# Up-weights of routed experts as one 8 KB run per partition, with gathered rows turned by every fourth column

## Chip, cores and metric

The kernel runs on one core of a Trainium2 chip. The metric is the device time of one execution in microseconds (us). Three runs of the kernel before gave 1488.46, 1491.83 and 1492.55 us, median 1491.83 us.

## What is computed

The reference is one step of a two-layer trunk over 640 tokens (512 latent and 128 context tokens) of 1024 features in float32. Layer 0 mixes tokens by latent attention and retention, layer 1 by a gated convolution. After each mixing follows a mixture of 32 experts, and only that part is touched by the change. A router picks 2 experts for each token, so 1280 rows go through experts. Cut to what matters:

```
def run(args):                                   # one block of rows, all of one expert
    xb, e = args
    a, b = jnp.split(xb @ w_up[e], 2, axis=-1)   # w_up[e]: 1024 x 512
    return (jax.nn.silu(a) * b) @ w_down[e]      # w_down[e]: 256 x 1024
```

Per layer the up-weights are 32 x 1024 x 512 and the down-weights 32 x 256 x 1024 float32 numbers: 2 MB and 1 MB for an expert.

## The kernel before, in words

**Order of the work.** Token mixing of layer 0, experts of layer 0, token mixing of layer 1, experts of layer 1. The program of each engine is written out by hand, with semaphores between them. The two expert stages lie at about 540 to 780 us and 1199 to 1440 us of the span; after each the rows of the experts are read back and summed per token.

**Rows.** The tokens' features are written to `h_rows` in HBM, two half rows of 512 numbers (2 KB) for a token. An expert's rows are cut into blocks of 64. For each block GpSimd (POOL) gathers 128 half rows by an indirect DMA into one of four places `land` (L2205): partition p holds the first half of row p, partition 64 + p the second half. VectorE (DVE) copies the place to `xrow` (L1950). TensorE (PE) turns it by four transposes of 128 columns each into PSUM (`turn_rows`, L937 to L941); DVE copies the result to `xblk` (L1955), where slice k holds the 128 features that meet row group k of the up-weights. In a transpose the turned data is the stationary operand, so it is read by the weight load (PEld L940), and the identity matrix moves.

**Experts.** For a block, `up` (L943) multiplies the eight slices of `xblk` by the expert's up-weights, two 64-column halves of the array side by side: 16 matmuls that the profile shows as 32 records of L955. Then come the four transposes of the next block, the eight records of the block before in `down` (L977), one transpose of the gated hidden values (`turn`, L965), and the next `up`. ScalarE (ACT) and DVE do the gate (L1443, L1516), ACT takes the result (L1454), and POOL scatters 128 half rows of it to `y_rows` (L2210). POOL's loop for a block waits for the gathered rows and gives a tick (L2200), waits for ACT's result, copies the two columns of indices, issues the gather two blocks ahead and the scatter of this block, and then waits until the scatter of the block before has landed (`freed`, which gives the other tick of L2200).

**Weights.** SyncE (SP) loads an expert by three DMAs of 1 MB: two of up-weights, 512 rows each (L488), and one of down-weights (L491), into three slots of 8 KB per partition. There are six such places. `refill` (L512 to L519) first waits until PE has done the last `up` of expert e, issues the two up-loads of expert e + 6 into its slots, then waits for its last `down` and issues the down-load. SP's DMAs go to one hardware queue, in the order of issue; POOL's go to a software queue; both are served by the same 16 DMA engines. PE waits for each of the three slots before it first reads it (L952, L971).

Before the change, partition p of an up-slot holds rows p, 128 + p, 256 + p and 384 + p of its 512 rows, four runs of 2 KB. A down-slot has two runs of 4 KB. The modulation weights `ada_w`, loaded in the first 250 us, are rows of 8 KB, one for a partition.

Of the kernel before, what the change touches and what calls it, by code (L numbers as in the profile page):

```python
# [12 lines left out]
P = 128  # L13
# [135 lines left out]
def build(nc, io):  # L149
    f = io  # L150
    ctx = ExitStack()
    with ctx:
# [3 lines left out]
        def sem(name):  # L156
            return ctx.enter_context(nc.semaphore(name))
# [42 lines left out]
        ident = cst[:, C_ID:C_ID + P]  # L200
# [50 lines left out]
        xrow = arena[:, A_XROW:A_XROW + HALFROW]  # L251
# [7 lines left out]
        def slot(s):  # L259

            if s < SLOTS:
                return ring[:, s, :]
            return arena[:, A_SLOT + (s - SLOTS) * SLOT:A_SLOT + (s - SLOTS + 1) * SLOT]
# [48 lines left out]
        ring_full = [sem(f"ring_full{s}") for s in range(SLOTS + MORE)]  # L312
        S = {}

        def ev(name):
            if name not in S:
                S[name] = sem(name)
            return S[name]
# [66 lines left out]
        def quad(b):  # L385
            return PS[:, b, :].rearrange("p (j n) -> p j n", j=4)
# [21 lines left out]
        def turned_bank(u):  # L408

            return 4 + 2 * (u % 2)  # L410
# [17 lines left out]
        def _(sp):  # L428
# [54 lines left out]
            def load_part(l, e, j, s):  # L483

                if j < 2:
                    src = f["moe_w_up"][l, bass.ds(e, 1), 512 * j:512 * j + 512, :] \
                        .rearrange("e (k p) n -> p (e k) n", p=P)
                    sp.dma_start(slot(s).rearrange("p (k n) -> p k n", k=4), src).then_inc(ring_full[s], 16)  # L488
                else:
                    src = f["moe_w_down"][l, bass.ds(e, 1), :, :].rearrange("e (k p) n -> p (e k) n", p=P)  # L490
                    sp.dma_start(slot(s).rearrange("p (k n) -> p k n", k=2), src).then_inc(ring_full[s], 16)  # L491

            def load_experts(l):
# [18 lines left out]
                def refill(e, p):  # L512

                    done = expert_done(e)
                    sp.wait_ge(ev(f"up_mm{l}"), done)
                    for j in range(2):
                        load_part(l, e + NPLACE, j, PLACES[p][j])
                    sp.wait_ge(ev(f"down_mm{l}"), done)
                    load_part(l, e + NPLACE, 2, PLACES[p][2])  # L519
# [12 lines left out]
            n = 0  # L532
# [16 lines left out]
        def _(pe):  # L549
# [55 lines left out]
            for g, r in enumerate(V_ROWS):  # L605
                last = pe.transpose(PS[:, 5, g * P:g * P + r], vrow[0:r, g, :], cst[0:r, C_ID:C_ID + r])
            last.then_inc(ev("vec_t"), 1)

            for i in range(2 * NT):
# [5 lines left out]
                for j in range(4):  # L615
                    last = pe.transpose(quad(i % 4)[:, j, :],
                                        xtok[:, t, (4 * half + j) * P:(4 * half + j + 1) * P], ident)
# [152 lines left out]
            for u in range(len(UNITS) + 2):  # L770
# [4 lines left out]
                if u < len(UNITS):  # L775
# [7 lines left out]
                    for half in range(2):  # L783
                        if kind == "q":
                            for k in range(2):
                                last = pe.matmul(PS[:, b + half, 0:384], cT[:, t, k, :],
                                                 wq[:, k, half * 384:half * 384 + 384],
                                                 start=(k == 0), stop=(k == 1))
                        else:
                            lat = cT[:, t, 2, :] if t < NT else cache_cT[:, :]  # L790
                            last = pe.matmul(PS[:, b + half, :], lat, wkv[:, half * 512:half * 512 + 512],
                                             start=True, stop=True)
                    last.then_inc(ev("qk_mm"), 1)
                if u >= 2:
# [10 lines left out]
                    for h in range(HEADS):  # L805
                        last = pe.transpose(quad(turned_bank(u - 2) + h // 4)[0:QK, h % 4, :], raw[:, h, :], ident)
# [7 lines left out]
            for i in range(NATT + 3):  # L814
                if i < NATT:
# [4 lines left out]
                    if kind == "lat":  # L820
                        for n in range(2):
                            last = pe.matmul(PS[:, b + n, 0:SEG], qT[:, h, t * P:t * P + P],  # L822
                                             kT[:, h, n * SEG:(n + 1) * SEG], start=True, stop=True)
                    else:
                        for n in range(4):
                            last = pe.matmul(quad(b)[:, n, :], qT[:, 4 * h + n, SAMPLE:T],
                                             kT[:, 4 * h + n, 640:768], start=True, stop=True)
                    last.then_inc(ev("s_mm"), 1)
                if 2 <= i <= NATT + 1:
# [6 lines left out]
                    for j in range(ST + 1 if kind == "lat" else 4):  # L836
                        last = pe.transpose(quad(4 + j // 4)[:, j % 4, :], prob[i % 2][:, j, :], ident)
                    last.then_inc(ev("p_t"), 1)
                if i - 3 in GROUP_END:
# [5 lines left out]
                    for pair in (range(2) if g < 2 else (0,)):  # L845
                        for j in range(ST + 1 if g >= 2 else 1):
                            for hl in range(2):
                                if g < 2:
                                    h = 4 * g + 2 * pair + hl
                                    out = PS[hl * VD:(hl + 1) * VD, 6 + g % 2, pair * P:(pair + 1) * P]  # L850
                                    last = pe.matmul(out, vS[:, 5, h, :],
                                                     probT[0][:, g, (2 * pair + hl) * P:(2 * pair + hl + 1) * P],
                                                     start=True, stop=True)
                                else:
                                    last = pe.matmul(PS[hl * VD:(hl + 1) * VD, 6 + g % 2, :],
                                                     vS[:, j, 2 * (g - 2) + hl, :], probT[hl][:, j, :],
                                                     start=(j == 0), stop=(j == ST))
# [3 lines left out]
            for t in range(NT):  # L861
# [4 lines left out]
                for j in range(4):  # L866
                    last = pe.transpose(quad(t % 4)[:, j, :], oret[:, t, j * P:(j + 1) * P], ident)
# [6 lines left out]
            def moe(l):  # L874
# [5 lines left out]
                for k in range(KD):  # L880
                    for n in range(2):
                        pe.wait_ge(ev("h_s"), KD // 2 + KD * (q - 1) + k + 1)
                        if n == 1:
                            pe.wait_ge(ev("h_c"), KD * (q - 1) + k + 1)
                        last = pe.matmul(PS[0:ROUTE, 5 * n, 0:SEG], wr[:, k, :], hT[:, k, n * SEG:(n + 1) * SEG],
                                         start=(k == 0), stop=(k == KD - 1))
# [24 lines left out]
                for i in range(2 * NT):  # L911
# [3 lines left out]
                    for j in range(4):  # L915
                        last = pe.transpose(quad((1, 2, 3, 7)[i % 4])[:, j, :],
                                            hT[:, 4 * half + j, t * P:t * P + P], ident)
# [7 lines left out]
                for j in range(2 * NT):  # L925
                    for h in range(2):
                        last = pe.matmul(PS[h * BLK:(h + 1) * BLK, 6, 0:NB], hot_lo[:, j, :], hot_hi[:, j, :],
                                         start=(j == 0), stop=(j == 2 * NT - 1))
# [6 lines left out]
                def turn_rows(n):  # L935

                    pe.wait_ge(ev(f"x_taken{l}"), n + 1)  # L937
                    pe.wait_ge(ev(f"xblk_c{l}"), n + 1)
                    for m in range(4):
                        last = pe.transpose(quad(3)[:, m, :], xrow[:, m * P:(m + 1) * P], ident)  # L940
                    last.then_inc(ev(f"rows_t{l}"), 1)  # L941

                def up(n, p, laps):  # L943
# [54 lines left out]
                def laps_at(g):  # L998

                    return lambda c: g * 16 + full_count[n0 + c]  # L1000

                turn_rows(0)
                up(0, 0, laps_at(0))
                with pe.Fori(0, rounds) as g:
# [117 lines left out]
            for k in range(KD):  # L1122
                pe.wait_ge(ev("ln_sq"), k + 1)
                for t in range(NT):
                    c = t * P if t < ST else CTX0
                    last = pe.matmul(PS[:, 0, t:t + 1], cv2[:, k, c:c + P], ones[:, 0:1],
                                     start=(k == 0 and t == 0), stop=(k == KD - 1 and t == NT - 1))
# [1210 lines left out]
```

## Time and profile before

| what | value |
|---|---|
| runs | 1488.46, 1491.83, 1492.55 us |
| the profiled execution's own time | 1487.51 us |
| its span, first to last instruction | 1485.7 us |
| mean granted TensorE clock | 0.941 |
| PE busy | 1285.3 us (87%) |
| DVE, ACT, POOL busy | 581.2, 296.3, 303.7 us |
| DMA packets, bytes | 149095, 322.65 MB |
| shares of the chain that ended last | PE 52%, DVE 15%, SP's queue 14%, DMA 7%, issue 7% |

The profile's times are of one execution. A share of an engine is an average over the whole span, and the stages have different limits, so the stages are read one by one. The "DMA share" of a stretch is the mean busy share of the 16 DMA engines; transfers that overlap on one engine can make it pass 1.

### The profile page before, as it was taken

The page shows a single profiled execution, that of the slowest core. Times are in us where ns is not written, and L with a number is a line of the kernel's source. Part 1 is how long each engine was busy: PE and PEld are TensorE (multiplying, and loading weights), DVE is VectorE, ACT ScalarE, POOL GpSimd, SP SyncE. Part 2 cuts the span into 40 slices and gives each one's busy share as a digit, 9 for nine tenths or more (in the row PEclk, how much of TensorE's full clock was granted, in tenths as well). Part 3 has the DMA queues.
Part 4 walks back from the last instruction along what each step waited for, and adds up shares of the span by engine and source line. Part 5 has one row for each costly group of instructions (what it writes and reads, how often), then busy time and mean ns, then how long its engine had stood idle before and what let it go on. Part 6 is the DMA issues. An engine that isn't in the chain of part 4 may idle for free.

```text
span 1485.7 us, 21303 instructions
## 1 busy us (share of the span) xinstructions
PE 1285.3 (87%) x7165; PEld 820.4 (55%) x7166; DVE 581.2 (39%) x1371; ACT 296.3 (20%) x653; POOL 303.7 (20%) x703
## 2 busy tenths in 40 slices
PE   4999998878799769997775899999898779999776
PEld 3666775554467445543334767666676445555336
DVE  1211433665422442221111379999412522222213
ACT  3300045554400311111111300000311311111110
POOL 3000100300000023443332211250000034444330
PEclk9999999979999769999997899999699679999998
DMA  9565645310061169999994811100071279999975
GB/s 339 232 277 230 267 180 230 122 55 1 1 255 57 71 208 401 412 408 400 404 356 167 246 57 31 54 29 0 0 278 62 89 270 398 386 400 411 404 281 218
DMA packets 149095, 322.65 MB, mean 217 GB/s; under 512 B 16182, under 2 KB 49948, under 8 KB 142884
## 3 DMA queue, kind: packets, MB, share of 16 engines
q1 hardware_dynamic: 128432, 288.25, 51.1%
q0 software_dynamic: 12464, 21.91, 4.2%
q10 hardware_dynamic: 8131, 11.57, 2.2%
q8 instruction: 45, 0.74, 0.2%
q14 instruction: 23, 0.18, 0.0%
HBM read 312.41 MB, written 27.08 MB: 229 GB/s over the span
## 4 chain that ended last, share of the span: by engine, by line
PE 52%; DVE 15%; SPq 14%; DMA 7%; issue 7%; ACT 3%; POOL 2%; ACTq 1%; POOLq 0%; DVEq 0%
PE PS L599 10%; PE PS L648 8%; DVE arena L2055 8%; PE PS L955 7%; SPq L491 7%; SPq L488 5%; PE PS L977 3%; DMA ring<-in_moe_w_up 3%; PE PS L1023 3%; PE PS L570 3%; PE PS L1082 2%; PE PS L822 2%; DVE scratch L1516 2%; DVE arena L1516 2%; PE PS L1099 2%
## 5 line engine op out<-in xcount | busy, mean ns | idle before, releaser
L1516 DVE TENSOR_TENSOR arena<-arena,PS 128x128 f32<-128x128 f32 (+1 forms) x101 | 33.4, 349 | 313.2 <-ACT arena L1443 304.2
L955 PE MATMUL PS<-arena 128*64 128x256 f32 x1152 | 134.7, 383 | 21.7 <-DMA arena<-in_moe_w_up 20.8
L2055 DVE SCALAR_TENSOR_TENSOR arena<-arena,vecT 128x655 f32<-128x655 f32 x181 | 151.0, 907 | 0.0
L955 PE MATMUL PS<-ring,arena 128*64 128x256 f32 x1056 | 129.0, 395 | 22.6 <-DMA ring<-in_moe_w_up 20.9
L599 PE MATMUL PS<-arena,ring 128*128 128x320 f32 x512 | 142.3, 442 | 5.7 <-DVE arena L1792 3.7
L1082 PE MATMUL PS<-arena,ring 128*128 128x320 f32 x512 | 141.4, 437 | 3.3 <-issue 2.2
L648 PE MATMUL PS<-ring,arena 128*128 128x256 f32 (+1 forms) x640 | 140.3, 372 | 0.0
L648 PEld LDWEIGHTS PS<-ring,arena 128*128 128x128 f32 x640 | 114.7, 190 | 26.7 <-issue 13.4
L599 PEld LDWEIGHTS PS<-arena,ring 128*128 128x128 f32 x512 | 99.4, 194 | 48.2 <-issue 8.9
L1082 PEld LDWEIGHTS PS<-arena,ring 128*128 128x128 f32 x512 | 98.3, 192 | 45.3 <-issue 5.6
L955 PEld LDWEIGHTS PS<-arena 128*64 128x64 f32 x1152 | 80.1, 137 | 65.1 <-DMA arena<-in_moe_w_up 17.5
L955 PEld LDWEIGHTS PS<-ring,arena 128*64 128x64 f32 x1056 | 76.3, 141 | 65.6 <-DMA ring<-in_moe_w_up 18.5
L1443 ACT ACTIVATE arena<-PS 128x128 f32<-128x128 f32 x69 | 19.1, 277 | 274.8 <-PE PS L955 274.8
L977 PE MATMUL PS<-arena 128*64 128x512 f32 x288 | 69.7, 605 | 1.5 <-ACT arena L1454 1.5
L2210 POOL DMA_INDIRECT y_rows<-arena,scatter_col x64 | 65.1, 1018 | 22.5 <-issue 22.5
L2281 POOL TENSOR_SCALAR arena<-cst,vecT 128x128 f32<-128x128 f32 x51 | 41.5, 830 | 124.3 <-PE PS L1099 124.3
L2100 POOL TENSOR_SCALAR arena<-arena,modA,modT 128x128 f32<-128x128 f32 x24 | 10.7, 449 | 274.2 <-DVE arena L1516 274.2
L1454 ACT ACTIVATE arena<-PS 128x512 f32 x61 | 36.4, 597 | 147.3 <-PE PS L977 147.3
L1023 PE MATMUL PS<-scratch,arena 128*128 128x128 f32 x320 | 42.1, 297 | 27.1 <-DMA arena<-y_rows 27.1
L2196 POOL TENSOR_TENSOR pool_tick<-cst 128x1 f32<-128x1 f32 x128 | 24.7, 193 | 198.5 <-ACT arena L1454 193.4
L2205 POOL DMA_INDIRECT arena<-h_rows,gather_col x56 | 59.3, 1058 | 28.3 <-issue 28.3
L977 PE MATMUL PS<-ring,arena 128*64 128x512 f32 x264 | 63.9, 605 | 0.0
(324 smaller groups left out, 1623.3 us busy)
## 6 DMA issues: line engine op xcount, KB each, us to landing
ring<-in_moe_w_up SPq DMA_DIRECT2D x64, 1024.0 KB, 13.8
arena<-in_moe_w_up SPq DMA_DIRECT2D x64, 1024.0 KB, 13.6
ring<-in_ada_w SPq DMA_DIRECT2D x48, 1024.0 KB, 10.9
ring<-in_moe_w_down SPq DMA_DIRECT2D x32, 1024.0 KB, 15.2
arena<-in_moe_w_down SPq DMA_DIRECT2D x32, 1024.0 KB, 15.2
arena<-y_rows ACTq DMA_DIRECT2D x10, 1024.0 KB, 11.1
ring<-in_od_w_in SPq DMA_DIRECT2D x16, 512.0 KB, 6.2
ring<-in_ev_w_in SPq DMA_DIRECT2D x7, 1024.0 KB, 14.9
```

The lines of the kernel that those rows point to most:

```text
L488: sp.dma_start(slot(s).rearrange("p (k n) -> p k n", k=4), src).then_inc(ring_full[s], 16)
L491: sp.dma_start(slot(s).rearrange("p (k n) -> p k n", k=2), src).then_inc(ring_full[s], 16)
L599: last = pe.matmul(PS[:, b + n, 0:SEG], w[:, k, c:c + P], src[:, tile(k), n * SEG:(n + 1) * SEG], start=(k == 0), stop=(k == KD - 1))
L648: last = pe.matmul(z_bank(i)[:, 0:n], hT[:, k, t * P:t * P + P], w[:, k, 0:n], start=(k == 0), stop=(k == KD - 1))
L955: last = pe.matmul(PS[i * BLK:(i + 1) * BLK, 0, 0:2 * P].rearrange("p (a n) -> p a n", a=2), xblk[:, k, :], w[:, k % 4, :, i * P:(i + 1) * P],
L977: last = pe.matmul(PS[c * BLK:(c + 1) * BLK, 2, :], hblk[:, i, :], w[:, i, c * 512:(c + 1) * 512], start=(i == 0), stop=(i == 1))
L1023: last = pe.matmul(quad(4 + i % 4)[:, m, :], ygat[:, t, a, c:c + P], wdiag[:, a, t, :], start=(a == 0), stop=(a == 1))
L1082: last = pe.matmul(PS[:, 2 * a + n, 0:SEG], w[:, k, a, :], hT[:, k, n * SEG:(n + 1) * SEG], start=(k == 0), stop=(k == KD - 1))
L1516: return dve.tensor_tensor(out, a, b, op)
L2055: dve.scalar_tensor_tensor(out=acc, in0=src, scalar=wc, in1=acc, op0=ALU.mult, op1=ALU.add).then_inc(ev("conv_v"), 1)
L2205: pool.indirect_dma_start(land[r], None, h_rows[:, :], bass.IndirectOffsetOnAxis(ap=col, axis=0), bounds_check=2 * T - 1, oob_is_err=False ...
L2210: pool.indirect_dma_start(y_rows[:, :], bass.IndirectOffsetOnAxis(ap=col, axis=0), yblk[r], None, bounds_check=2 * ROWS - 1, oob_is_err=Fa ...
```

## The change

An up-slot's partition p now holds rows 4p to 4p + 3 of its 512 rows, which stand next to each other in HBM: one run of 8 KB. The 1 MB of a DMA is then one piece of HBM. For the products to stay what they are, slice m of a block has to hold the features 4c + m instead of 128m + c, so each transpose reads every fourth column of `xrow`. Nothing else is changed: the same number of DMAs, bytes, transposes and matmuls, and the same waits.

```diff
@@ load_part (SP)
                 if j < 2:
                     src = f["moe_w_up"][l, bass.ds(e, 1), 512 * j:512 * j + 512, :] \
-                        .rearrange("e (k p) n -> p (e k) n", p=P)
-                    sp.dma_start(slot(s).rearrange("p (k n) -> p k n", k=4), src).then_inc(ring_full[s], 16)
+                        .rearrange("e (p k) n -> p (e k n)", p=P)
+                    sp.dma_start(slot(s), src).then_inc(ring_full[s], 16)
@@ turn_rows (PE)
                     for m in range(4):
-                        last = pe.transpose(quad(3)[:, m, :], xrow[:, m * P:(m + 1) * P], ident)
+                        last = pe.transpose(quad(3)[:, m, :], xrow.rearrange("p (c m) -> p m c", m=4)[:, m, :], ident)
                     last.then_inc(ev(f"rows_t{l}"), 1)
```

## Rows read from the trace of the kernel before

**Rows 1.** Windows: busy time (instructions) per engine, granted clock, DMA share, GB/s.
```profile
580.00:660.00 80.00, 80.00 (x576) 41.41 (x574) 19.97 (x51) 11.86 (x38) 39.59 (x104) 1.00 1.04 410
660.00:760.00 100.00, 74.96 (x510) 37.23 (x508) 18.06 (x47) 11.29 (x35) 34.23 (x93) 1.00 1.04 401
...
1220.00:1260.00 40.00, 40.00 (x294) 20.88 (x292) 9.51 (x24) 5.79 (x18) 16.82 (x40) 1.00 1.03 392
1340.00:1380.00 40.00, 40.00 (x292) 20.64 (x290) 9.51 (x24) 5.79 (x18) 19.78 (x53) 1.00 1.04 410
1380.00:1420.00 40.00, 30.83 (x210) 14.88 (x208) 7.92 (x20) 4.82 (x15) 14.42 (x40) 1.00 1.04 405
```

**Rows 2.** Groups of instructions, PE line L955: busy, mean ns, idle before, releasers.
```profile
L955 PE MATMUL PS<-arena 128*64 128x256 f32 x1152 | 134.7, 383 | 21.7 <-DMA arena<-in_moe_w_up 20.8 <-DVE arena L1955 0.9
L955 PE MATMUL PS<-ring,arena 128*64 128x256 f32 x1056 | 129.0, 395 | 22.6 <-DMA ring<-in_moe_w_up 20.9 <-issue 1.7
```

**Rows 3.** The chain that ended last, in order of time: start, us, what.
```profile
577.17 1.89 PE PS L977 x8
579.22 3.08 SPq L491
...
762.75 15.50 DMA arena<-in_moe_w_up
778.29 1.95 PE PS L955 x16
...
1320.28 4.65 SPq L491
```

**Rows 4.** Timeline of SP, the last down-load issued in each expert stage.
```profile
765.47 3.55 SPq L491 DMA_DIRECT2D arena<-in_moe_w_down  x1
...
1425.55 3.47 SPq L491 DMA_DIRECT2D arena<-in_moe_w_down  x1
```

**Rows 5.** Windows in which runs of one length alone are loaded (columns as rows 1).
```profile
145.00:155.00 10.00, 10.00 (x60) 7.04 (x59) 2.62 (x6) 0.38 (x1) 0.00 (x0) 1.00 1.01 424
...
298.00:300.00 2.00, 1.05 (x8) 0.83 (x8) 1.43 (x4) 1.25 (x4) 0.00 (x0) 0.90 1.04 403
300.00:302.00 2.00, 0.42 (x2) 0.44 (x3) 2.00 (x3) 0.70 (x2) 0.00 (x0) 0.50 1.01 412
437.00:441.00 4.00, 4.00 (x17) 2.81 (x16) 0.00 (x0) 0.00 (x0) 0.00 (x0) 1.00 1.00 372
441.00:443.00 2.00, 2.00 (x9) 1.42 (x8) 0.55 (x2) 0.00 (x0) 0.00 (x0) 1.00 1.06 430
549.00:553.00 4.00, 4.00 (x32) 2.23 (x30) 1.30 (x3) 0.28 (x1) 0.63 (x1) 1.00 1.04 400
```

**Rows 6.** Page, part 3, SP's and POOL's queue: packets, MB, share of 16 engines.
```profile
q1 hardware_dynamic: 128432, 288.25, 51.1%
q0 software_dynamic: 12464, 21.91, 4.2%
```

**Rows 7.** Line L940, the weight loads of the transposes: ns min/median/max, first and last start.
```profile
L940 PEld LDWEIGHTS PS<-cst,arena x284: 137/140/230, 537.8 to 1440.1; 128*128 128x128 f32 x142
```

**Rows 8.** Windows around the first of these transposes (columns as rows 1).
```profile
537.00:539.00 2.00, 1.09 (x4) 0.71 (x4) 0.47 (x2) 0.00 (x0) 1.36 (x3) 0.50 0.00 0
```

**Rows 9.** Timeline of POOL, one block of layer 0.
```profile
620.53 1.02 POOL L2210 DMA_INDIRECT y_rows<-arena,scatter_col  x1 [0.30 <-issue]
621.57 0.35 POOL L2200 TENSOR_TENSOR pool_tick<-cst 128x1 f32<-128x1 f32 x2
624.27 0.19 POOL L2196 TENSOR_TENSOR pool_tick<-cst 128x1 f32<-128x1 f32 x1 [2.35 <-ACT arena L1454]
...
627.88 0.35 POOL L2200 TENSOR_TENSOR pool_tick<-cst 128x1 f32<-128x1 f32 x2
```

**Rows 10.** Line L2210, the scatters: issue to landing.
```profile
DMA to landing us min/median/max: 2.1/5.8/7.8
```

**Rows 11.** Line L2106, POOL's small loads beside the first 4 and 8 KB runs.
```profile
DMA to landing us min/median/max: 6.7/8.7/9.6
```

## The prediction

> **What bounds the kernel now.** The page first: PE is busy for 87% of the span, but that mixes stages, so I went to windows of the two expert stages, the only ones the change touches. From 580 to 660 us PE is busy without a gap and the DMA engines are full too (share 1.04, 410 GB/s). From 660 to 760 us the DMA engines stay full and PE is busy 75 of 100 us. Layer 1 shows the same later: PE has no gap up to 1380 us and then 9 us of gaps in 40 [rows 1]. The groups of instructions name what PE waits for: in front of the up matmuls it idles 20.8 + 20.9 = 41.7 us for `moe_w_up` [rows 2]. 25 us of gaps lie between 660 and 760 us, 9 us between 1380 and 1420 [rows 1], and the rest right behind these, so some 29 us in layer 0 and 12.7 us in layer 1. The chain of waits gives the start: up to 579 us it runs through PE, from there through SP's issues, which are held back by a full queue, to the landing of the last up-weights at 778.3 us, where PE takes them at once; in layer 1 it leaves PE at 1320 us [rows 3]. So both stages begin bound by PE (6.32 us a block: POOL's tick comes at 621.57 and 627.88 [rows 9]) and end bound by the DMA engines. SP's timeline has 21 down-loads after 579.2 us, the last at 765.5 us, and 12 after 1320.3 us, the last at 1425.6 us [rows 3, 4]: they come 8.9 and 8.8 us apart on average.
>
> **Part 1, the up-loads.** 128 loads of 1 MB keep their bytes; 512 packets each become 128, so SP's queue drops from 128432 packets [rows 6] by 128 x 384 = 49152 to about 79280. What a packet costs comes from stretches in which one length of run is loaded. 2 KB runs: 403, 372 and 400 GB/s; 4 KB runs: 412 and 430; 8 KB runs of `ada_w`: 424 [rows 5]. I take 400, 412 and 424, because they rebuild the stage: 2.097 MB at 400 is 5.24 us, 1.049 MB of down-weights at 412 is 2.55 us, and POOL's queue, 21.91 MB over 64 experts [rows 6] or 0.34 MB for one, takes 0.84 us at 400: 8.63 us, against 3.49 MB / 401 = 8.70 by the stage's own rate [rows 1]. With 8 KB runs the up part is 2.097 / 424 = 4.95 us, **0.30 us less for an expert** that the DMA engines bound. Bounds: if the whole loss of 401 against 424 GB/s over 3.49 MB lay in the up-runs, they would give back 8.70 - 8.23 = 0.47 us, of which I keep 0.43, since the 4 KB runs lose some too. Below, the stage shows 410 with the same mix while PE is full [rows 1]; a fixed cost per packet that fits 410 and 424 is some 4 ns, times 48 fewer packets on each engine, 0.19 us. Zero, or a loss, is a rival.
>
> The Trainium skill (DMA: Bandwidth & Descriptors, Why small descriptors are slow) gives about 3 cycles a packet beside one cycle per 32 bytes. By it, as an estimate, an up-load would go from 67/64 to 259/256 of its ideal time, 3.4% less, or 0.18 us an expert. No row here shows that mechanism by itself.
>
> Which experts count? Those that the DMA engines bound: 21 in layer 0 and 12 in layer 1, and in each the two whose loads are queued at the turning point (a load lands 15.5 us after its issue [rows 3], close to two services): 23 + 14 = 37. Bounds 33 (none of the queued) and 42 (share 1.03 already from 1220 us [rows 1], which the faster engines would partly turn into idle time). **37 x 0.30 = 11.1 us**; from 33 x 0.19 = 6 to 42 x 0.43 = 18. It can't be eaten by the floor beneath: layer 0 would lose 6.9 of 29 us of PE gaps, layer 1 4.2 of 12.7. At the end nothing new is late, as the last up-load is still followed by the same matmuls, scatter and read-back.
>
> SP issues as many DMAs as before. Their long issue times are the full queue's; with a quarter of the packets I expect SP to be held back less and more bytes to stand in the queue, so that issue to landing may get longer than now. That costs nothing: the order in the queue is the same, and an expert's slots are free when SP issues. The first six experts of a stage are loaded long before they are needed, so their gain is nothing.
>
> **Part 2, the transposes.** There are 2208 / 32 = 69 blocks [rows 2], 33 in layer 0 and 36 in layer 1, with four transposes each, and what is strided is the weight load: 128 numbers per partition at a step of 16 bytes. A load takes 140 ns now [rows 7]. No row shows a strided float32 operand on PE. From below the price is zero (a gain has no source: same bytes, same count). From above: the slowest load, 230 ns [rows 7], is of the first block, where the granted clock is 0.50, that is 1.2 GHz [rows 8]; a load whose reads go at half rate can hardly lose more than one that goes at half clock, 90 ns. Times four that is 0.36 us a block. It lies on the path only where PE bounds: (579 - 540) / 6.32 = 6 blocks of layer 0 and (1320 - 1199) / 6.32 = 19 of layer 1. That is 25 x 0.36 = 9.0 us at most; in the other blocks the gaps in front of the up matmuls cover it, and without that cover all 69 blocks would pay 25 us. I take zero: nearest are the plain loads of the same line at full clock, and the 140 ns hold more than the reading of 128 columns (they don't double at half clock).
>
> **Sum.** 0 to 9 us for the transposes, 11.1 off for the loads. On the profiled execution 1487.5 - 11 = 1476.5 us. That execution lies 4.3 us below the median of the three runs, and the sum applied to the median gives **1481 us**. Its own range is 1474 to 1486.
>
> **Rivals.**
> *The strided loads go at half rate.* For it: every column lies 16 bytes from the next. Against it: nothing in the trace. The price is between 4.4 us (half of the bound) and 9.0, so the change gains 2 to 7 us: 1487, range 1484 to 1490. At over 0.44 us a block, 110 ns a load, it would eat the whole gain. The Trainium skill (SBUF — State Buffer, Door 1) speaks against this change: lines of SBUF are 16 bytes, and at least two reads of each line are needed for full rate, where a step of four float32 numbers gives one. By that rule, this rival is the result.
>
> *Not the packet's length but the memory limits the rate.* For it: 2 and 4 KB runs overlap (403 and 412), one 4 KB stretch reaches 430, beyond the 8 KB runs [rows 5]. The `ada_w` rows come from other addresses than one solid megabyte. Then the change does not do what it says: 1492, or 1491 to 1497 with a part of the transposes' price.
>
> *Slower: the software queue is starved.* An engine that takes turns between queues waits longer behind an 8 KB packet. Scatters land in 5.8 us beside the weights and in 2.1 us at best [rows 10], so the neighbours cost 3.7 us. The mean packet of SP's queue takes (64 x 82 + 16 x 159) / 80 = 97 ns on an engine now and (16 x 309 + 16 x 159) / 32 = 234 ns after, 2.4 times. If the extra scales with it, a scatter lands after 2.1 + 8.9 = 11.0 us. POOL's slack is 9.7 us: 7.35 from the issue at 620.53 to the tick at 627.88, which waits for nothing, and 2.35 in which it then idles for ACT [rows 9]. From 9.7 us on POOL sets the pace. I take 0.8 us a block, a landing of 10.5 us, between the slack and that: layer 1 becomes 36 x 7.12 = 256 us against its 241 now, and layer 0, 33 x 7.12 = 235 and 2 for the first block at 1.2 GHz, against 240: 12 us slower, 1504. Below about 0.5 us a block, a landing of 10.2 us, the gain of layer 0 makes up for layer 1. Against it: POOL's small loads beside 4 and 8 KB runs at the start took 8.7 us, at most 9.6, with others of their own queue ahead of them [rows 11]; and landings in the expert stages vary little though 2 and 4 KB runs alternate. The Trainium skill (DMA: Bandwidth & Descriptors, Queues, rings and completion order) has each engine change queues at packets only, which is the rule behind this rival.
>
> **Chances.** Forecast 0.50, half-rate loads 0.25, rate unchanged 0.15, starved software queue 0.10. A measurement of this kernel tells about 0.3%, 4.5 us, from no change. Faster by more: 0.48 of the forecast and 0.11 of the second. Within it: 0.02, 0.14 and 0.12. Slower: 0.03 and 0.10. The range runs from the forecast's lower end over the half-rate and most of the unchanged case, 1474 to 1493.
>
> **What would show it.** SP's queue with about 79280 packets. In 660:760 us some 415 GB/s, and down-loads 8.3 us apart. The gaps for `moe_w_up` near 31 us instead of 41.7. PEld of L940 at 140 ns; 180 to 230 is the half-rate rival, with blocks of 6.5 to 6.7 us while PE is full. Scatters landing under 9.7 us; above, POOL idles in front of its tick L2200 for `y_rows`. The prediction is wrong if up-loads alone don't pass 410 GB/s, or if a stage without gaps on PE gets longer.

## The result, and the profile after

The changed kernel takes 1480.63 us in the median of five runs (1476.77 to 1482.74), the kernel before 1492.55 us beside it (1488.46 to 1495.46, five runs). The ratio is 0.9916, with a 95% interval of 0.9895 to 0.9937: **some 12 us faster** (11.9 by the medians, 12.5 by the ratio). The profiled execution took 1476.77 us (span 1474.9) where the one of before took 1487.51.

The page of after, part 3, for the two queues of [rows 6] (packets, MB, share of 16 engines):

```profile
q1 hardware_dynamic: 79280, 288.25, 49.3%
q0 software_dynamic: 12464, 21.91, 4.2%
```

49152 packets are gone from SP's queue, the bytes are the same, and the same bytes took less of the engines' time: 51.1% before. The windows of after that answer to [rows 1], with a new one for 1260 to 1300 us:

```profile
580.00:660.00 80.00, 80.00 (x571) 42.53 (x567) 19.26 (x48) 11.83 (x38) 38.55 (x102) 1.00 1.02 422
660.00:760.00 100.00, 82.32 (x554) 42.47 (x552) 20.55 (x51) 11.86 (x37) 37.64 (x99) 1.00 1.02 423
...
1260.00:1300.00 40.00, 40.00 (x284) 21.29 (x282) 9.91 (x25) 6.06 (x19) 19.57 (x50) 1.00 0.95 367
1340.00:1380.00 40.00, 40.00 (x283) 21.25 (x283) 9.92 (x25) 6.47 (x20) 18.54 (x50) 1.00 1.02 423
1380.00:1420.00 40.00, 34.04 (x235) 17.30 (x231) 8.02 (x20) 4.82 (x15) 16.35 (x43) 1.00 1.02 422
```

Where the DMA engines are full they now move 422 to 423 GB/s, whatever PE does; before it was 401 to 410. That is the rate of the 8 KB `ada_w` runs, 424 [rows 5]. PE is busy 82.3 us of the hundred where it was 75.0. What it still waits for stands in the groups of L955 (busy, mean ns, idle before), against 20.8 and 20.9 us for `moe_w_up` in [rows 2]:

```profile
L955 PE MATMUL PS<-arena 128*64 128x256 f32 x1152 | 134.2, 383 | 13.0 <-DMA arena<-in_moe_w_up 11.8 <-DVE arena L1955 1.1
L955 PE MATMUL PS<-ring,arena 128*64 128x256 f32 x1056 | 126.1, 389 | 17.5 <-DMA ring<-in_moe_w_up 15.9 <-issue 1.7
```

The gaps fell from 41.7 to 27.7 us. The transposes' line shows the other side (ns min/median/max); [rows 7] had 137/140/230:

```profile
L940 PEld LDWEIGHTS PS<-cst,arena x284: 195/212/226, 538.7 to 1430.3; 128*128 128x128 f32 x142
```

A weight load with a step of 16 bytes takes 212 ns, 72 ns more. It is hidden in part: POOL's timeline of after, to be read beside [rows 9], has its ticks 6.42 and 6.38 us apart where they were 6.31.

```profile
615.96 0.34 POOL L2200 TENSOR_TENSOR pool_tick<-cst 128x1 f32<-128x1 f32 x2
618.75 0.19 POOL L2196 TENSOR_TENSOR pool_tick<-cst 128x1 f32<-128x1 f32 x1 [2.45 <-ACT arena L1454]
...
621.33 1.02 POOL L2210 DMA_INDIRECT y_rows<-arena,scatter_col  x1 [0.30 <-issue]
622.38 0.34 POOL L2200 TENSOR_TENSOR pool_tick<-cst 128x1 f32<-128x1 f32 x2
...
628.76 0.36 POOL L2200 TENSOR_TENSOR pool_tick<-cst 128x1 f32<-128x1 f32 x2
```

So a block costs PE 0.09 to 0.10 us more (four loads of 72 ns would be 0.29; two thirds lie beside matmuls). The tick at 622.38 still follows the scatter's issue at once, and POOL still idles 2.45 us for ACT: the scatters are not late here. Over both expert stages, POOL waited for a scatter's landing in front of L2200 three times, 1.5 us in all, where it was twice and 0.7 us before.

The chain that ended last (start, us, what) leaves PE later than in [rows 3], at 611.5 instead of 579.2 us, and in layer 1 at 1344.6 instead of 1320.3:

```profile
609.45 1.89 PE PS L977 x8
611.50 1.89 SPq L491
...
748.04 23.67 DMA arena<-in_moe_w_up
771.76 1.95 PE PS L955 x16
...
1344.60 2.23 SPq L488
...
1379.82 24.68 DMA ring<-in_moe_w_up
```

The last up-load of layer 0 lands at 771.8 us (778.3 before). It takes 23.7 us from issue to landing instead of 15.5: at 423 GB/s that would be 10.0 MB ahead of it in the queue, against 6.2 MB at 401 (an estimate, rate times time).

**The stages in numbers.** The chain gives two marks for each layer: the router's matmuls L927 in front of the experts and the sums L1023 behind them. First before, then after:

```profile
527.05 2.41 PE PS L927 x40
803.05 9.85 PE PS L1023 x64
1186.01 2.41 PE PS L927 x40
1455.11 9.79 PE PS L1023 x64
```

```profile
528.88 2.41 PE PS L927 x40
796.62 8.89 PE PS L1023 x64
1181.18 2.42 PE PS L927 x40
1445.38 8.78 PE PS L1023 x64
```

From L927 to L1023 layer 0 goes from 276.0 to 267.7 us, layer 1 from 269.1 to 264.2: **8.3 and 4.9 us**, together 13.2. The other stretches, which the change does not touch, add up to 2.4 us more in this execution (1.8 before the first mark, 1.6 between the layers, 1.1 less at the end). Over the ten other profiles of this study whose code there is the same, the first mark lies between 530.2 and 533.2 us, so a few us in one execution mean nothing there; the two stage lengths are the better measure, and I use them below. They have noise too: where two or three profiles have the same code in a layer, the lengths differ by 0.4 to 1.4 us, and once, with one of the doubled kernels below, by 2.2. So a difference of about 1 us between two single profiles says little.

### The profile page after: what moved, and what is told of

Its sections match the earlier page's. It is cut to its first block, busy times and chain, and to the rows that moved or that the text cites. A ratio compares the mean times of both kernels' runs of the same rounds, so it can differ in the third digit from the quotient of the medians.

```text
span 1474.9 us, 21303 instructions
## 1 busy us (share of the span) xinstructions
PE 1289.7 (87%) x7165; PEld 831.6 (56%) x7166; DVE 582.5 (39%) x1371; ACT 296.3 (20%) x653; POOL 304.0 (21%) x703
## 3 DMA queue, kind: packets, MB, share of 16 engines
q1 hardware_dynamic: 79280, 288.25, 49.3%
## 4 chain that ended last, share of the span: by engine, by line
PE 57%; DVE 15%; SPq 9%; DMA 8%; issue 6%; ACT 3%; POOL 2%; ACTq 1%; POOLq 0%; DVEq 0%
PE PS L599 10%; PE PS L955 9%; PE PS L648 8%; DVE arena L2055 8%; SPq L488 5%; PE PS L977 4%; DMA ring<-in_moe_w_up 3%; SPq L491 3%; PE PS L1023 3%; PE PS L570 3%; PE PS L1082 2%; PE PS L822 2%; PE PS L940 2%; DVE scratch L1516 2%; DMA arena<-in_moe_w_up 2%
## 5 line engine op out<-in xcount | busy, mean ns | idle before, releaser
L955 PE MATMUL PS<-arena 128*64 128x256 f32 x1152 | 134.2, 383 | 13.0 <-DMA arena<-in_moe_w_up 11.8
L955 PE MATMUL PS<-ring,arena 128*64 128x256 f32 x1056 | 126.1, 389 | 17.5 <-DMA ring<-in_moe_w_up 15.9
L955 PEld LDWEIGHTS PS<-arena 128*64 128x64 f32 x1152 | 80.3, 137 | 55.5 <-DMA arena<-in_moe_w_up 10.9
L955 PEld LDWEIGHTS PS<-ring,arena 128*64 128x64 f32 x1056 | 75.1, 139 | 58.8 <-DMA ring<-in_moe_w_up 13.9
L977 PE MATMUL PS<-arena 128*64 128x512 f32 x288 | 69.7, 605 | 1.5 <-ACT arena L1454 1.5
L2210 POOL DMA_INDIRECT y_rows<-arena,scatter_col x64 | 65.1, 1018 | 22.4 <-issue 22.4
L940 PE MATMUL PS<-cst,arena 128*128 128x128 f32 x284 | 53.8, 313 | 14.9 <-DVE arena L1950 14.9
L1023 PE MATMUL PS<-scratch,arena 128*128 128x128 f32 x320 | 41.8, 296 | 27.2 <-DMA arena<-y_rows 27.2
L977 PE MATMUL PS<-ring,arena 128*64 128x512 f32 x264 | 63.9, 605 | 0.0
```

Of the source, the lines that this page charges most:

```text
L940: last = pe.transpose(quad(3)[:, m, :], xrow.rearrange("p (c m) -> p m c", m=4)[:, m, :], ident)
L955: last = pe.matmul(PS[i * BLK:(i + 1) * BLK, 0, 0:2 * P].rearrange("p (a n) -> p a n", a=2), xblk[:, k, :], w[:, k % 4, :, i * P:(i + 1) * P],
L977: last = pe.matmul(PS[c * BLK:(c + 1) * BLK, 2, :], hblk[:, i, :], w[:, i, c * 512:(c + 1) * 512], start=(i == 0), stop=(i == 1))
L1023: last = pe.matmul(quad(4 + i % 4)[:, m, :], ygat[:, t, a, c:c + P], wdiag[:, a, t, :], start=(a == 0), stop=(a == 1))
L2210: pool.indirect_dma_start(y_rows[:, :], bass.IndirectOffsetOnAxis(ap=col, axis=0), yblk[r], None, bounds_check=2 * ROWS - 1, oob_is_err=Fa ...
```

## The experiments

Three questions were open. Does the gain come from the packet's length or from the solid megabyte? What does the strided read cost, and on which stretch is it paid? And which resource sets the end of a stage in which PE and the DMA engines are both full? None leaves any of the computation out; two do transposes twice. The kernel before was measured beside each set of kernels: 1492.17 us beside the first four (23 runs), 1493.74 beside the next four (11 runs), 1492.77 beside the last two (21 runs). "+/-" gives a 95% interval of a difference of means.

### The order made by VectorE

```diff
@@ take_landed (DVE), on the changed kernel
-                    dve.tensor_copy(xrow, src)
+                    dve.tensor_copy(xrow.rearrange("p (m c) -> p m c", m=4),
+                                    src.rearrange("p (c m) -> p m c", m=4))
@@ turn_rows (PE)
-                        ... xrow.rearrange("p (c m) -> p m c", m=4)[:, m, :], ident)
+                        ... xrow[:, m * P:(m + 1) * P], ident)
```

> The kernel after, but DVE's copy of the gathered rows (L1950) puts every fourth column side by side, so that the transposes read 128 columns in one run again; 8 KB runs as after. Theory A, the strided weight load costs PE 0.09 us a block (a block takes 6.41 us after, 6.32 before) and only the PE-bound blocks count (about 29 to 45 of 69): 3 to 4 us faster than after, 14 to 16 us faster than before, L940's loads back at 140 ns and a block at 6.32 us. Theory B, the load's extra 72 ns are hidden behind the other operand's work and the 0.09 us come from something else: no change against after, 12 us faster than before. In both DVE's copy may take 0.2 to 0.4 us longer, beside DVE's idle time.

Measured: 1479.46 us (1476.69 to 1481.87, six runs), ratio 0.9916 (0.9901 to 0.9931). Its line L940 and its groups of L955 (one line lower in the code):

```profile
L940 PEld LDWEIGHTS PS<-cst,arena x284: 137/140/230, 542.0 to 1432.4; 128*128 128x128 f32 x142
```

```profile
L955 PE MATMUL PS<-arena 128*64 128x256 f32 x1152 | 134.5, 383 | 16.7 <-DMA arena<-in_moe_w_up 15.9 <-DVE arena L1956 0.9
L955 PE MATMUL PS<-ring,arena 128*64 128x256 f32 x1056 | 126.0, 389 | 18.2 <-DMA ring<-in_moe_w_up 16.1 <-issue 2.2
```

The loads are back at 140 ns, the block at 6.32 us, so the strided load is where the 0.09 us came from, against theory B. DVE's copy L1950 went from a mean of 421 to 624 ns, and no wait for it grew (PE 15.3 us in all, at the first blocks of the two stages, where it was 16.9 in the kernel before). The median is 1.2 us under the changed kernel's, too little to tell the two theories' times apart. The gaps for up-weights are 32.0 us instead of 27.7: of the 69 x 0.09 = 6.2 us that PE saves, 4.3 turn into waiting. Layer 0's stage is 267.6 us long, as in the changed kernel, and layer 1's 263.3 instead of 264.2.

### The stride alone

```diff
@@ take_landed (DVE), on the kernel before: loads stay four runs of 2 KB
-                    dve.tensor_copy(xrow, src)
+                    dve.tensor_copy(xrow.rearrange("p (c m) -> p m c", m=4),
+                                    src.rearrange("p (m c) -> p m c", m=4))
@@ turn_rows (PE)
-                        ... xrow[:, m * P:(m + 1) * P], ident)
+                        ... xrow.rearrange("p (c m) -> p m c", m=4)[:, m, :], ident)
```

> The kernel before, with its 2 KB runs, but the transposes read every fourth column (DVE's copy spreads the rows so that the products stay the same). Theory A: the stride alone makes a block 6.41 us where PE has no gap, that is 25 to 30 blocks on the path: 2 to 3 us slower than before, 1494 to 1496 us, and the DMA engines stay at 401 to 410 GB/s. Rival (half-rate loads at the full price of 0.29 to 0.36 us a block): 7 to 9 us slower. Rival (hidden): same as before.

Measured: 1493.69 us (1490.9 to 1496.14, twelve runs), ratio 1.001 (1.0001 to 1.002), so 1.5 us slower, and no more than 3. L940 loads take 212 ns here too. Layer 0's stage is 276.3 us (276.0 before), layer 1's 270.3 (269.1). The 25 blocks that the prediction counted as bound by PE, at 0.09 us each, would be 2.3 us, inside the interval. The full price of 0.29 to 0.36 us a block is not.

### Short packets over the same megabyte

```diff
@@ load_part (SP), on the changed kernel
-                        .rearrange("e (p k) n -> p (e k n)", p=P)
-                    sp.dma_start(slot(s), src)
+                        .rearrange("e (p k) n -> p (e k) n", p=P)
+                    sp.dma_start(slot(s).rearrange("p (k n) -> p k n", k=4)[:, ::-1, :], src)
@@ turn_rows (PE)
-                        ... [:, m, :], ident)
+                        ... [:, 3 - m, :], ident)
```

The four rows of a partition are written in reverse order, so that a packet can't be longer than 2 KB though the addresses read are those of the changed kernel.

> The kernel after with the same bytes in the same partitions, but each partition's 8 KB taken as four runs of 2 KB (their order in the slot reversed, so that they can't be joined, and the transposes reversed with it). Theory A, what is gained is the packets' fixed cost: SP's queue has 128432 packets again, the full stretches fall from 423 back to 400 to 410 GB/s, and the time is that of before plus the stride's 2 to 3 us, 1494 us. Rival, the addresses make it (one solid megabyte instead of rows 256 KB apart): 423 GB/s and 1481 us in spite of the packets.

Measured: 1491.82 us (1489.91 to 1496.47, twelve runs), ratio 1.0001 (0.9988 to 1.0013). Its queue and windows:

```profile
q1 hardware_dynamic: 128432, 288.25, 50.6%
```

```profile
580.00:660.00 80.00, 80.00 (x559) 41.88 (x555) 20.48 (x51) 11.85 (x37) 36.54 (x96) 1.00 1.04 411
660.00:760.00 100.00, 79.29 (x540) 41.11 (x540) 19.26 (x48) 11.58 (x36) 36.55 (x96) 1.00 1.04 404
```

**The gain is gone**, with the rates of before. The packet's length makes it, not where the bytes lie. A us or two may still come from the solid megabyte: the kernel with the stride alone, which like this one reads every fourth column, took 1493.69 us, in the means 1.1 +/- 1.6 us more, and its stages are 276.3 and 270.3 us long against 274.7 and 269.4 here. That is not shown.

### Two runs of 4 KB

```diff
@@ load_part (SP), on the changed kernel
-                        .rearrange("e (p k) n -> p (e k n)", p=P)
-                    sp.dma_start(slot(s), src)
+                        .rearrange("e (k p j) n -> p (e k) (j n)", k=2, j=2)
+                    sp.dma_start(slot(s).rearrange("p (k n) -> p k n", k=2), src)
@@ turn_rows (PE)
-                        ... xrow.rearrange("p (c m) -> p m c", m=4)[:, m, :], ident)
+                        ... xrow.rearrange("p (k c j) -> p k j c", k=2, j=2)[:, m // 2, m % 2, :], ident)
```

> Up-weights as two runs of 4 KB per partition; the transposes read every second column, a step of 8 bytes. Theory A, a fixed cost per packet: from 2 to 8 KB an engine's 64 packets of an expert's up-weights become 16 and 0.45 us are saved, so with 32 packets two thirds, 0.30 us: full stretches near 415 to 418 GB/s, 4 us slower than after by the loads. Rival, packets pay only beyond 4 KB or only up to 4 KB: 403 or 423 GB/s. For the stride: if a line of 16 bytes must be hit twice, a step of 8 bytes is free and L940's loads take 140 ns and a block 6.32 us; if the load time grows with the step, some 165 to 175 ns and 6.36 us.

Measured: 1481.87 us (1477.04 to 1482.92, six runs), ratio 0.9925 (0.9908 to 0.9941). Windows and the line of the transposes:

```profile
580.00:660.00 80.00, 80.00 (x560) 41.93 (x561) 20.86 (x52) 12.21 (x38) 36.57 (x96) 1.00 1.03 419
660.00:760.00 100.00, 81.00 (x552) 41.93 (x548) 19.25 (x48) 11.63 (x37) 38.23 (x101) 1.00 1.03 418
```

```profile
L940 PEld LDWEIGHTS PS<-cst,arena x284: 194/209/226, 541.9 to 1434.0; 128*128 128x128 f32 x142
```

4 KB runs bring most of it: 401 to 418 GB/s, then 423 with 8 KB. The time can't be told from the changed kernel's (1480.63). And a step of 8 bytes costs a load 209 ns, as good as a step of 16.

### The down-weights as one 8 KB run too, and the step that it needs

```diff
@@ load_part (SP), on the kernel with DVE's order
-                    src = f["moe_w_down"][...].rearrange("e (k p) n -> p (e k) n", p=P)
-                    sp.dma_start(slot(s).rearrange("p (k n) -> p k n", k=2), src)
+                    src = f["moe_w_down"][...].rearrange("e (p k) n -> p (e k n)", p=P)
+                    sp.dma_start(slot(s), src)
@@ up (PE): the moving operand takes every second column
-                        w = slot(s[k // 4]).rearrange("p (k a n) -> p k a n", k=4, a=2)
+                        w = slot(s[k // 4]).rearrange("p (k a n i) -> p k a i n", k=4, a=2, i=2)
-                                xblk[:, k, :], w[:, k % 4, :, i * P:(i + 1) * P],
+                                xblk[:, k, :], w[:, k % 4, :, i, :],
```

> DVE's copy orders the columns as in e1_dve_order, and the down-weights too land as one 8 KB run per partition; the up matmuls then read every second column of the up-weights as their moving operand, so that slice k of the hidden values meets rows 2p + k. SP's queue should show 79280 - 16384 / 2 = 71088 packets. If packet length goes on paying above 4 KB, the expert stages go from 423 to about 425 GB/s where the DMA engines are full, 0.04 us for an expert and 1 to 2 us in all, if the strided moving operand is free. Theory one (the gain is used up near 4 KB, as 419 GB/s with 4 KB up-runs and 423 with 8 KB suggest, and a strided moving operand costs nothing that PE cannot hide): 1478 to 1480 us, the same as with contiguous transposes alone. Rival (the moving operand is read at a lower rate at a step of 8 bytes): the up matmuls of 256 columns go from about 0.24 us for two to more, 16 of them for each block; at 0.02 us each that is 0.3 us for each of some 25 blocks that PE bounds, or 8 us, 1487 us.

The second kernel keeps the step but writes the down-weights' two rows in swapped order, so the packets stay at 4 KB, and `down` reads them swapped:

> As f1_down_8k, with the down-weights in the same layout but written as two 4 KB runs per partition in swapped order, so that packets stay at 79280 and only the moving operand's step is new against e1_dve_order. If the strided moving operand is free: 1479 us, as e1_dve_order, and the difference of f1_down_8k to this one is the packets' alone. If it costs something, both kernels show it alike in the mean ns of L955 and in the block's period while PE is full.

Measured: 1479.46 us (1476.63 to 1484.41, six runs), ratio 0.9906 (0.9883 to 0.9929), with the 8 KB down-runs (71088 packets); 1483.36 us (1478.26 to 1486.87, six runs), ratio 0.993 (0.9906 to 0.9954), with the step alone (79280). The window of 660 to 760 us, first with both and then with the step alone:

```profile
660.00:760.00 100.00, 85.30 (x573) 41.27 (x569) 23.39 (x52) 12.54 (x39) 39.41 (x104) 1.00 1.01 425
```

```profile
660.00:760.00 100.00, 84.65 (x569) 40.79 (x567) 23.29 (x52) 12.56 (x39) 38.79 (x104) 1.00 1.02 423
```

Neither theory holds alone. The packets pay a little if at all (425 against 423 GB/s; stages 1.0 and 0.7 us shorter, the whole kernel 3.1 +/- 3.6 us in the means), and the step is not free: `down` L977 comes every 6.49 us instead of 6.32 while PE is full, 0.17 us a block, and the stages are 1.2 and 2.4 us longer than the mean of the two profiles with DVE's order. The kernel with the step alone is 5.7 +/- 3.1 us slower than DVE's order measured beside it (1477.16, next section), the one with both 2.5 +/- 3.0. So the kernel is no better than the one that it was built on.

### Both candidates once more, on the same chip

> The kernel of e1_dve_order once more, beside the changed kernel on the same chip, since the two differ by less than one measurement tells. If the strided weight loads lie on the path of some 25 to 35 blocks at 0.09 us, this kernel is 2 to 3 us faster than the changed one. If PE only arrives earlier at weights that have not landed, the difference is under 1 us.

> The changed kernel once more, on the same chip as the three others: 1480.6 us again. It is what f3_dve_order_again is compared with: 2 to 3 us slower than that one if the strided loads lie on the path, within 1 us if not.

Measured: 1477.16 us (1476.09 to 1479.33, five runs), ratio 0.9893 (0.9871 to 0.9915), with DVE's order; 1479.72 us (1477.95 to 1482.93, six runs), ratio 0.9911 (0.989 to 0.9933), changed kernel. All runs of each kernel together: mean 1478.5 (11 runs) against 1480.4 (11 runs). With a spread of about 1.9 us in either group the difference is 1.9 us, give or take 1.7. The six and five runs made side by side give 2.9 +/- 2.2. **DVE's order is the fastest version found**, by about 2 us. The stages don't show where: averaged over two profiles of each, layer 0 loses 0.7 us (268.3 against 267.6) and layer 1 gains 0.9 (263.0 against 263.9), 0.2 together, and the profiled executions themselves average 1478.0 and 1478.3 us.

### Twice the transposes, one layer at a time

```diff
@@ turn_rows (PE), on the changed kernel; in the other kernel l == 1
-                    for m in range(4):
+                    for m in [m for _ in range(2 if l == 0 else 1) for m in range(4)]:
```

> The changed kernel, with the four transposes of a block done twice over in layer 0: the same results are written again, so each block of layer 0 costs PE 0.66 to 0.75 us more (the quad takes 0.75). Theory one: a stage's end is set by the DMA engines from the moment their share stays at 1 or above, in layer 0 from about 565 us, although PE has no gap until 607. Then only the 3 or 4 blocks before that count, which release the first new loads: +2 to +3 us, layer 0's expert stage 267.6 to some 270, and the rest of the cost vanishes as smaller gaps in front of the up matmuls. Theory two: PE sets the end until the chain of waits leaves it at 609 us: 11 blocks, +7 to +8 us.

> The same doubling in layer 1 alone. There the DMA share is 0.92 to 0.97 between 1260 and 1300 us and stays at 1.02 from 1300 on, so PE's pace sets when SP may load until then. Theory one: the 17 blocks between 1193 and 1300 us count at 0.66 to 0.75 us, +11 to +13 us, layer 1's stage 264 to some 276, a little less if the share reaches 1 earlier or later by it. Theory two: 23 blocks until the chain leaves PE at 1340 us, +15 to +17 us. Common to both theories and telling against a third (transposes are never on the path): layer 1 pays far more for the same instructions than layer 0.

Measured: layer 0 doubled 1486.26 us (1482.47 to 1490.83, ten runs), ratio 0.9964 (0.995 to 0.9978); layer 1 doubled 1492.12 us (1488.04 to 1496.3, twelve runs), ratio 0.9998 (0.9985 to 1.0011). So 6 and 12 us more than the changed kernel. PE's timeline with layer 0 doubled shows what it costs a block:

```profile
605.55 1.94 PE L977 MATMUL PS<-arena 128*64 128x512 f32 x8
612.44 1.94 PE L977 MATMUL PS<-arena 128*64 128x512 f32 x8
```

6.89 us instead of 6.41: 0.48 us for four more transposes, not the 0.66 to 0.75 that both theories were given (part of a transpose hides behind its neighbours when eight come in a row). The marks of both, first layer 0 doubled:

```profile
531.57 2.41 PE PS L927 x40
803.30 10.05 PE PS L1023 x64
```

```profile
1183.64 2.41 PE PS L927 x40
1458.69 10.14 PE PS L1023 x64
```

Layer 0's stage takes 271.7 us, 4.0 more than the 267.7 that it takes in the twin kernel where only layer 1 is doubled. Layer 1's takes 275.1, 11.1 more than the mean of 264.2 and 263.6. If every block paid, it would be 33 x 0.48 = 16 and 36 x 0.48 = 17 us. Layer 0 pays for 8 blocks, layer 1 for 23.

For layer 0 that lies between the theories: one had 3 to 4 blocks, 1.4 to 1.9 us at the measured 0.48, and two had 11, 5.3 us. The whole kernel's 6.2 +/- 2.3 us over the changed kernel run again excludes the first count and not the second. The 8 fit the windows if "full" is read by the rate and not by the share, a reading made after the result: 377 GB/s from 560 to 580 us in this kernel, 424 from 580. About 0.6 us of the 4.0 come behind the last landing (25.5 us from there to L1023 instead of 24.9), and the seven blocks left end at 541.5 + 7 x 6.89 = 590 us.

What speaks against theory two is where the chain leaves PE in these two profiles. With layer 1 doubled, layer 0 runs the changed kernel's own code, and its stage is 267.7 us long as there, but the chain stays with PE until 663 us instead of 611:

```profile
657.00 1.87 PE PS L977 x8
659.13 3.95 PE PS L955 x32
664.68 2.47 SPq L488
```

A point that moves by 52 us and leaves the stage's length as it is does not mark the start of the critical stretch. With layer 0 doubled the chain leaves PE at 676.6 us, 20 blocks after the start, and 20 x 0.48 = 9.4 us is more than either measure shows.

For layer 1 neither count can be read off as it was meant, because the doubling moves the point itself:

```profile
1260.00:1300.00 40.00, 40.00 (x291) 22.86 (x289) 9.37 (x24) 5.64 (x18) 18.40 (x48) 1.00 0.93 355
1340.00:1380.00 40.00, 40.00 (x286) 22.28 (x286) 9.34 (x23) 5.52 (x17) 17.45 (x48) 1.00 1.02 423
1380.00:1420.00 40.00, 40.00 (x284) 22.38 (x282) 9.63 (x24) 5.79 (x18) 17.36 (x47) 1.00 1.02 423
```

PE has no gap up to 1420 us and the DMA engines run below capacity until 1320. The 11.1 us are the 17 minus some 6 us of gaps that the doubling filled (PE idles 6.0 us between 1380 and 1420 us in the changed kernel). What stands: the same extra instructions cost nearly three times as much in layer 1 as in layer 0 by the stages, and twice as much by the whole kernel (12.0 against 6.2 us).

The doubled layer 0 leaves 2 us unexplained: its run is some 6 us longer and its stage 4.0. In its profile the untouched stage of layer 1 took 265.8 us, where the changed kernel's two profiles have 264.2 and 263.6. The cause stays open.

## Why the prediction was right, and where its steps were off

The prediction was 1481 us, the measurement 1480.63; the forecast drop was 11.1 us, the measured one 11.9. Part of that agreement is luck: two errors against each other.

**What bounds the kernel.** Right in kind: the gain lies in the expert stages (8.3 and 4.9 us), and it comes from the stretches where the DMA engines are full.

**Packets.** 79280, as counted.

**0.30 us for an expert: too small.** The step that was off is the term "400, 412 and 424". The text expected some 415 GB/s between 660 and 760 us and gaps for `moe_w_up` near 31 us; it got 423 and 27.7. An expert's 3.49 MB take 8.25 us at 423 GB/s. Against the 8.70 us at 401 that is 0.45 us less, beyond the text's own upper bound of 0.43. Against the 8.51 us at 410, which held in the first 80 us, it is 0.26. The text kept some of the loss for the 4 KB down-runs, but those lose almost nothing: with the down-runs at 8 KB as well the rate rises only from 423 to 425. The four lengths give the price of a packet in place of that sum. Removing 32, 16 and 8 packets on each engine for an expert took the stage from 410 to 419, 422 and 424 GB/s where PE is full, which is 0.18, 0.06 and 0.04 us: 4 to 6 ns a packet, near the 4 ns that the text had fitted for its lower bound. Between 660 and 760 us the first step, from 2 to 4 KB, brought 0.35 us, 11 ns a packet. Why 2 KB packets lose more there (401 to 404 GB/s in three kernels, share 1.04) is open.

The rule of the Trainium skill (DMA: Bandwidth & Descriptors, Why small descriptors are slow) gave 0.18 us an expert as an estimate. The right direction, and less than the 0.26 to 0.45 us measured here.

**37 experts: near enough, for another reason than given.** The text started the count where the chain of waits leaves PE. The chain left PE 32 and 24 us later after the change, yet the gain did not shrink, and that point moves by itself, as the doubling shows. What fits is a count from when the DMA engines of the changed kernel run at capacity: about 580 us in layer 0, 1300 in layer 1, PE's gaps or not. These starts were read off after the result. Then the bytes alone give the gain. In layer 0 the kernel before moved 80 us x 410 + 100 us x 401 = 72.9 MB between 580 and 760 us; at 422.6 GB/s that takes 172.5 us, 7.5 less, and some 0.8 for the 18 us to the last landing: 8.3, as measured. In layer 1, if one starts at 1300 us, the kernel before moved 390 and 412 GB/s for 20 us each (its windows below) and 410 and 405 for 40 us each. That is 48.6 MB, 5.0 us less at 423, and some 0.8 to 1440 us: 5.8. Measured were 4.9 with the stride and 6.1 with DVE's order.

```profile
1300.00:1320.00 20.00, 20.00 (x142) 9.90 (x138) 5.22 (x13) 2.89 (x9) 9.22 (x24) 1.00 1.03 390
1320.00:1340.00 20.00, 20.00 (x146) 10.46 (x146) 5.05 (x13) 3.58 (x11) 9.20 (x25) 1.00 1.05 412
```

The kernel before does not show that start: its share is 1.02 or more from 1220 us on. Counted from there, with 373, 411, 401 and 376 GB/s up to 1300 us, the gain would be 12 us, twice what was measured. Only in the changed kernel do the engines fall below capacity from 1260 to 1300 us (share 0.95), probably because the faster engines then wait for PE's pace: with PE slowed by the doubling in layer 1 they stay below it until 1320 us. The prediction had that in its upper bound of 42 experts.

**SP held back less, landings longer.** Right: 23.7 and 24.7 us against 15.5.

**Transposes at zero: wrong in kind, small in effect.** The text took 140 ns, "nearest are the plain loads of the same line"; they took 212. That is most of the way to the bound of 230, and the load does not hide: 0.09 us a block while PE is full. The half-rate rival asked for a block of 6.5 to 6.7 us and got 6.41. What kept it cheap is the second half of the bound, the 25 blocks: about 8 of layer 0 count, as doubling them shows, and PE's loss elsewhere only fills gaps. By price, 8 + 17 blocks at 0.09 us (the 17 being those of layer 1 up to 1300 us) would be 2.3 us; the whole-kernel comparison gives 1.9 +/- 1.7 us, the stride alone on the kernel before 1.5. The stage lengths give 0.2 in the first comparison and 1.5 in the second.

**Sum.** In place of -11.1 and 0: about -14 for the loads (8.3 + 5.8, an estimate), +1 to +2 for the stride; the median fell by 12 (1492.55 to 1480.63).

**The rivals.** *Half-rate loads:* the loads took 212 ns, inside the 180 to 230 of this rival; the time did not follow. The rule behind it (the Trainium skill, SBUF — State Buffer, Door 1: at least two reads of each 16-byte line for full rate) does not fit the runs: a step of 8 bytes makes two reads of a line and costs 209 ns, a step of 16 makes one and costs 212; contiguous is 140. *Rate unchanged:* refuted by the 8 KB rows, and its argument (addresses) by the short packets over the same megabyte. *Starved software queue:* refuted as a cause of time. POOL's tick follows the scatter's issue at once, and it still idles 2.45 us for ACT. So the scatters land inside the 9.7 us of slack, but for the few waits of 1.5 us in all, though the mean packet beside them is 2.4 times as long by the prediction's estimate. The rule behind it (the Trainium skill, DMA: Bandwidth & Descriptors, Queues, rings and completion order: an engine changes queues at packets only) may hold; no run here shows it by itself.

## What to carry to other kernels

Where the windows show the DMA engines full, count packets first: going from 2 KB to 4 KB runs was worth 2 to 4% of the rate, 4 to 8 KB one more per cent. If the layout then asks for a permutation, look for an engine with slack in a copy that is done anyway; here DVE's copy took it for 200 ns that no wait grew by. And when two resources are both full, don't take the start of the critical stretch from the chain of waits: it moved by 52 us here between two executions whose stage was equally long. Price the stretch by bytes over rate, and keep a wide range for where it starts, since that depends on where the changed kernel first runs at its capacity, which the kernel before need not show.

## What the runs showed of the hardware that was not expected

- A strided float32 weight load takes 209 ns at a step of 8 bytes and 212 at 16, against 140 contiguous (128 columns, 2.4 GHz). Of the 4 x 72 = 288 ns that four such loads cost more, 0.09 us reach the block's period.
- A moving operand of float32 at a step of 8 bytes costs too: the two-by-128-column matmuls of L955 went from a mean of 383 to 391 ns, 0.17 us for 16 matmuls.
- A full queue held more bytes with longer packets: some 6.2 MB before (15.5 us to landing at 401 GB/s), some 10.0 MB after (23.7 us at 423), and with 8 KB runs throughout the up-load of layer 1 on which PE last waited took 29.9 us to land.
- From 580 to 660 us neither PE nor the DMA engines had a gap, and yet PE's pace mattered little: 0.48 us more in every block of layer 0, 16 us in all, made the stage 4.0 us longer, while 422 instead of 401 to 410 GB/s made it 8.3 us shorter.
